# Prompt attention interleaved over four tiles, the routing table made on TensorE, and w_in asked in the phase before

## The chip, the cores and the metric

One core of one Trainium2 chip runs the whole program. The metric is the device time of one execution in microseconds; lower is better. PE is TensorE, DVE VectorE, ACT ScalarE, POOL GpSimd, and SP issues transfers.

## What is computed

One inference step of a trunk of two layers, for a prompt of 2048 tokens and eight samples of one token. Layer 0 is sparse attention: an indexer of 8 heads scores every earlier key, each query keeps its 256 best keys, and 16 query heads over 4 key heads attend to those. Layer 1 is a recurrent block. A mixture of experts follows each: of 4 groups one is chosen, in it 2 of 8 experts. Everything is f32. Cut to what the change touches:

```python
def indexer_scores(qi, wi, ki, q_pos, k_pos):
    dots = jnp.einsum('bqhd,bsd->bqhs', qi, ki)
    s = jnp.einsum('bqhs,bqh->bqs', jax.nn.relu(dots), wi * IDX_SCALE)
    return jnp.where(k_pos[None, None, :] <= q_pos[None, :, None], s, -jnp.inf)
# per block of 128 queries: _, idx = lax.top_k(sc, 256); attention over k[idx], v[idx] only

def dispatch_experts(x, eidx, ew, w1, w2):   # eidx: two experts per token
    order = jnp.argsort(flat_e)
    padded = (counts + blk - 1) // blk * blk          # each expert filled up to blocks of 128
    dest = pstart[se] + (jnp.arange(A) - start[se])
    row_tok = jnp.full((nb * blk,), N, jnp.int32).at[dest].set(st)
    xb = x_pad[row_tok].reshape(nb, blk, D)           # rows by block, gathered
```

## The kernel before

The program is a chain of phases, each a block in which the five queues run their own instruction lists in order and meet by semaphores; a barrier stands between two phases. The order is `phase_modulation`, `phase_project`, `phase_attend`, `phase_sample_index`, `phase_sample_attend`, then for layer 0 `phase_route`, `phase_experts`, `phase_combine`, then `phase_recurrent`, then the last three again for layer 1.

`phase_modulation` (L133) multiplies the condition with 12 slabs of 2 MB of `ada_w` (SP asks them at L170, four buffers). `phase_project` (L258) multiplies 17 tiles of 128 tokens with `w_in`; POOL asks for that weight at L312 as the phase opens, while SP asks for the modulation, the rope table (L299, L300), a gain and then the tiles x (L306).

`phase_attend` (L484) treats 16 tiles of 128 queries in order; tile t sees 128(t + 1) keys. No key is gathered: the indexer's score is kept for all keys, a search by bits (31 counts over the row, `counted`, L752) finds the 256th largest, and a bf16 row `hide` of 0 or a large negative number is added to the logits through a product with an identity. One turn of the loop for tile t has these parts, and each queue holds them in this order:

- *maxima*: PE makes the logits in bf16 (L838 adds `hide`, L839 the product) for 16 heads in units of up to 1024 keys, in two halves of `big` (four PSUM banks); DVE takes the maximum of each (L788), then `negmax` (L790).
- *index of tile t + 1*: PE turns the index queries (L812) and makes dots in pairs of pieces of up to 512 keys (L820) into the two banks of `dots`; ACT rectifies (L649), DVE weighs and adds to `score` (L724, L728). DVE first runs `normalise(t - 1)` (L710, L712).
- *projection of tile t - 1*: PE, 32 instructions (L909) into `big`; ACT copies (L694), POOL multiplies by the gate, adds x and stores.
- *turning the queries of tile t + 1* (L901), copied by ACT (L658) and narrowed to bf16 by POOL (L594).
- *products of tile t*: PE takes two blocks of 128 keys at a time, each for the 4 heads of one key head: `hide` and `negmax` by products (L866, L867), the f32 logits (L872), two blocks later the product with V (L887) into `po` or `dots`. ACT takes the exponential (L681). ACT copies results out in `copy_out` (L674).
- beside them DVE runs the *search of tile t + 1*; the mask (L743, L745) waits until the products of tile t have read the old `hide`.

`phase_route` (L1345) norms each token tile, multiplies with the router and, when all are done, DVE computes for each token its two places in the list sorted by expert (`dest`, L1610). POOL writes the token numbers to `row_tok` in DRAM with 34 indirect transfers (L1464). `phase_experts` (L1671) loads that list back (L1745), casts it (L1807), turns it on PE (L1875) and copies it (L1809); from it POOL gathers the rows of each block (L1752).

## Time and profile before

| | |
|---|---|
| median of 3 runs | 6822.19 us (6815.61 to 6827.62) |
| the profiled execution | 6845.33 us |
| its span, first to last instruction | 6843.7 us |
| PE, PE weight loads, DVE, ACT, POOL busy | 74%, 36%, 41%, 21%, 10% |
| mean granted clock of TensorE | 0.823 |
| DMA | 634 MB, mean 93 GB/s |

A row of a table of stretches gives a stretch in us from the span's start, its length, for each of PE, PE weight loads, DVE, ACT and POOL the busy us with the instructions in brackets, then the mean granted clock, the busy share of the DMA engines and GB/s. A row of a timeline gives start, length, engine (SPq is SP's queue), line, operation, output and inputs, shape, how many instructions are merged, and in square brackets the idle time of that engine before it and what ended it. Matmul ends are modelled; the distance between two starts is the surer figure.

### The profile page before, as it was taken

What the parts mean: (1) busy time and instruction counts of PE and PEld (TensorE: products, weight loads), DVE (VectorE), ACT (ScalarE), POOL (GpSimd) and SP (SyncE); (2) the same over time, 40 slices, a digit from 0 to 9 for tenths busy, and PEclk for the clock granted to TensorE, in tenths of its full rate; (3) what the DMA queues carried; (4) which work ended last, traced back from release to release, by engine and by line L of the source; (5) the groups of instructions that cost most, each with busy time, mean ns of one, the idle gap of its engine ahead of it and who ended that gap; (6) DMA issues with size and microseconds to landing.
All of it is one profiled execution on the core that took longest, in us unless ns stands there. A gap on an engine that the chain in (4) does not pass through costs nothing. (4 is left out here: it accounts for less than half of the span.)

```text
span 6843.7 us, 59514 instructions
## 1 busy us (share of the span) xinstructions
PE 5063.8 (74%) x16273; PEld 2487.8 (36%) x16274; DVE 2836.4 (41%) x5054; ACT 1432.4 (21%) x2686; POOL 714.1 (10%) x943
## 2 busy tenths in 40 slices
PE   6999678888888888874376479962888886559970
PEld 1444223222223322322033334432656565424430
DVE  1111688866677786501812301114444442311014
ACT  0111222222222222220021112211323221212221
POOL 0111110000000000000021210111000000120013
PEclk8999788877799888985687589985899896579985
DMA  6111100000000000003243567754010000437865
GB/s 224 54 50 38 64 12 22 11 12 11 11 11 11 11 11 7 7 8 106 81 146 106 204 227 282 269 213 173 19 37 18 31 19 11 147 105 256 293 225 165
DMA packets 197327, 634.38 MB, mean 93 GB/s; under 512 B 49533, under 2 KB 68353, under 8 KB 178572
## 3 DMA queue, kind: packets, MB, share of 16 engines
q1 hardware_dynamic: 129454, 404.10, 17.2%
q0 software_dynamic: 41888, 136.49, 5.9%
q10 hardware_dynamic: 25824, 91.88, 3.3%
q8 instruction: 72, 1.18, 0.1%
q14 instruction: 89, 0.73, 0.0%
HBM read 497.55 MB, written 134.89 MB: 92 GB/s over the span
## 5 line engine op out<-in xcount | busy, mean ns | idle before, releaser
L1861 PE MATMUL experts_ps_gu<-w_sb,experts_xT 128*128 x1504 | 682.5, 608 | 42.1 <-DMA w_sb<-moe_w_in 37.7
L752 DVE TENSOR_SCALAR_CACHE_REDUCE attend_relu<-attend_score,attend_cand 128x384 f32<-128x384 f32 (+13 forms) x448 | 662.7, 1479 | 43.4 <-issue 3.1
L2373 PE MATMUL recurrent_psAB<-recurrent_hT,rec_w_in_sb 128*128 128x256 f32 (+1 forms) x2304 | 536.1, 392 | 10.6 <-ACT recurrent_hT L2168 10.6
L468 PE MATMUL project_pj<-project_w,project_hT 128*128 128x512 f32 (+2 forms) x1360 | 507.9, 531 | 6.6 <-ACT project_proj L384 5.5
L2373 PEld LDWEIGHTS recurrent_psAB<-recurrent_hT,rec_w_in_sb 128*128 128x128 f32 x2304 | 463.7, 215 | 76.9 <-issue 11.7
L681 ACT ACTIVATE attend_PT<-attend_big 128x512 f32<-128x512 f32 x544 | 297.1, 595 | 631.0 <-PE attend_big L872 629.9
L1861 PEld LDWEIGHTS experts_ps_gu<-w_sb,experts_xT 128*128 128x128 f32 x1504 | 286.2, 195 | 373.2 <-issue 373.2
L820 PE MATMUL attend_dots<-kiT,attend_qiT 64*128 64x512 f32 (+3 forms) x640 | 267.2, 930 | 202.8 <-ACT attend_relu L649 191.8
L838 PE MATMUL attend_big<-attend_hide,attend_identb 128*128 128x512 bf16 (+3 forms) x640 | 259.1, 406 | 180.1 <-DVE attend_mx L788 94.2
L788 DVE TENSOR_REDUCE attend_mx<-attend_big 128x1 f32<-128x1024 f32 (+7 forms) x384 | 334.4, 909 | 126.2 <-PE attend_big L839 121.8
L1851 PE MATMUL experts_ps_y<-w_sb,experts_midT 128*128 x752 | 343.1, 599 | 11.4 <-issue 11.4
L1815 DVE SCALAR_TENSOR_TENSOR experts_th<-experts_th,experts_ps_gu 128x256 f32<-128x256 f32 x94 | 39.6, 421 | 731.1 <-ACT experts_th L1789 731.1
L468 PEld LDWEIGHTS project_pj<-project_w,project_hT 128*128 128x128 f32 (+1 forms) x1360 | 229.5, 185 | 262.0 <-issue 254.9
L872 PE MATMUL attend_big<-attend_qT,KT 64*128 64x512 f32 x1088 | 307.2, 641 | 0.0
L887 PE MATMUL attend_po<-attend_PT,V 128*128 128x512 f32 x544 | 269.8, 618 | 0.0
L909 PE MATMUL attend_big<-attend_w_out,attend_oT 128*128 128x512 f32 x512 | 253.2, 657 | 20.2 <-DVE attend_oT L712 20.2
L887 PE MATMUL attend_dots<-attend_PT,V 128*128 128x512 f32 x544 | 266.0, 615 | 0.0
L2404 PE MATMUL recurrent_psO<-rec_w_out_sb,recurrent_g 128*128 128x512 f32 (+1 forms) x544 | 240.0, 602 | 28.9 <-DVE recurrent_g L2330 28.9
L728 DVE SCALAR_TENSOR_TENSOR attend_score<-attend_relu,attend_wi,attend_score 128x512 f32<-128x512 f32 (+3 forms) x280 | 187.4, 671 | 165.4 <-ACT attend_relu L649 146.7
L839 PE MATMUL attend_big<-attend_KTb,attend_qTb 128*128 128x512 bf16 (+3 forms) x640 | 252.2, 406 | 0.0
L649 ACT ACTIVATE attend_relu<-attend_dots 128x512 f32<-128x512 f32 (+3 forms) x320 | 154.8, 531 | 317.7 <-PE attend_dots L820 260.2
L820 PEld LDWEIGHTS attend_dots<-kiT,attend_qiT 64*128 64x128 f32 x640 | 74.3, 283 | 385.4 <-ACT attend_relu L649 369.7
(372 smaller groups left out, 6285.5 us busy)
## 6 DMA issues: line engine op xcount, KB each, us to landing
w_sb<-moe_w_in SPq DMA_DIRECT2D x64, 2048.0 KB, 11.8
w_sb<-moe_w_in SPq DMA_DIRECT2D x64, 1024.0 KB, 8.7
yb_scratch<-experts_y ACTq DMA_DIRECT2D x94, 512.0 KB, 8.6
modulation_slab<-ada_w_in SPq DMA_DIRECT2D x12, 2048.0 KB, 9.4
index_slab<-ada_w_in SPq DMA_DIRECT2D x12, 2048.0 KB, 8.2
sample_V<-cache_v_in POOLq DMA_DIRECT2D x128, 128.0 KB, 2.4
sample_K<-cache_k_in SPq DMA_DIRECT2D x128, 128.0 KB
route_x<-xa_scratch SPq DMA_DIRECT2D x32, 512.0 KB, 4.5
```

The lines of the kernel that those rows point to most:

```text
L468: last = pe.matmul(pj[0:rows, bank, 0:c1 - c0], hT[:, b, k, 0:rows], w[:, k, c0:c1], start=(k == 0), stop=(k == KC - 1))
L681: act.activation(PT[:, k % 4, :], big[:, k % 4, :], ACT.Exp).then_inc(exped, 1)
L752: dve.tensor_scalar(relu[:, :, :].rearrange("p a n -> p (a n)")[:, 0:w], score[:, 0:w], bound, 0.0, op, ALU.add, accum_out=count[:, :])
L788: dve.tensor_reduce(mx[:, h, u:u + 1], flat[:, 1024 * (k % 2):1024 * (k % 2) + wide], AX.X, ALU.max).then_inc(maxed, 1)
L820: pe.matmul(dots[:, k % 2, 0:keys.stop - keys.start], qiT[r, h // 2, :], kiT[r, keys], start=True, stop=True).then_inc(dotted, 1)
L838: pe.matmul(bank, identb4[:, 0, :], hide[:, keys], start=True, stop=False)
L872: pe.matmul(big[:, k % 4, :], KT[r, n // 2, b * P:(b + 1) * P], qT[r, t % 2, n // 2 * GQ:(n // 2 + 1) * GQ, :].rearrange("p a q -> p (a q) ...
L887: pe.matmul(out_bank(n), V1[:, b, n, :], PT[:, k % 4, :], start=(b == 0), stop=(b == per - 1)).then_inc(pv_done, 1)
L909: last = pe.matmul(big[:, 2 + half, :], oT[:, k, :], w_out[:, k, half * 512:half * 512 + 512], start=(k == 0), stop=(k == KC - 1))
L1851: last = pe.matmul(ps_y[:, half, :], midT[:, k, :], w2[:, bass.ds(slot, 1), k, half * 512:half * 512 + 512].rearrange("p a n -> p (a n)"), ...
L1861: last = pe.matmul(ps_gu[:, u, :], xT[:, u, k, :], w1[:, bass.ds(slot, 1), k, :].rearrange("p a n -> p (a n)"), start=(k == 0), stop=(k == ...
L2373: last = pe.matmul(psAB[:, c % 2, part, 0:W], w_in[:, k, part * D + c * P:part * D + (c + 1) * P], hT[:, k, 0:W], start=(k == 0), stop=(k ...
```

## The change

- **Attention.** The tiles are taken in the order 0, 1, 3, 5, ... 15, 14, 12, ... 2. Step i of the new loop (`steps`, -3 to 16) holds four tiles: the products of the i-th, the maxima of the next, the search of the one after, the index dots of the third. The step is divided in slots of two product blocks (`slots`, 2(t + 1) of them). Units of the maxima, now 512 keys wide in the two banks `aux`, are dealt over the first half of the slots, pairs of index pieces over the second half, and 33 rounds of the search over all; in the middle slot stand the normalising and projection of the tile before and the turning of index queries, behind the last slot the turning of queries. `hide` has three buffers, `score` and `diag` two, `qT` three. `aux` serves maxima, turning, dots and projection; `po` all products with V. The count of the search writes its elements to the bf16 tile `passed`. `qi_rows` and `q_rows` of the first tile are asked before `w_out`, and all engines wait for the constants first.
- **w_in.** The weight has a tile that lives through modulation and projection, and SP asks for it behind the last slab. Three of the four slabs lie in `V1` and `KT`.
- **Routing table.** DVE splits each place into block and row, marks both as 0 or 1 (times the token number), and PE multiplies 34 pairs of marks, which sums to the table of token numbers by row and block; DVE copies it to `idx`, which stays in SBUF. The `row_tok` list, its fill, scatters, load and turn go, in both layers.

```diff
@@ phase_modulation
+        slab = [pair[:, 0], pair[:, 1], T["KT"]..., slab3[:, :, :]]
+                for k in range(KC):
+                    sp.dma_start(T["project_w"][:, k, :], T["attn_w_in"][k * P:(k + 1) * P, :]).then_inc(T["project_w_in"], 16)
@@ phase_project
-                for k in range(KC):
-                    pool.dma_start(w[:, k, :], T["attn_w_in"].rearrange("(k p) n -> p k n", p=P)[:, k, :]).then_inc(w_in, 16)
-                    pool.wait_ge(w_in, 16 * KC)
@@ phase_attend
+        TILE = [0] + list(range(1, NT, 2)) + list(range(NT - 2, 0, -2))
+        ROUNDS = 33
+        def steps():
+            return range(-3, NT + 1)
+        def slots(i):
+            return S[i] // 2 if there(i) else 1
+        def share_of(n, s, first, last):
+            if not first <= s < last:
+                return range(0)
+            s, of = s - first, last - first
+            return range(n * s // of, n * (s + 1) // of)
+        def units_at(i, s):
+            return share_of(U[i + 1], s, 0, max(middle(i), 1)) if there(i + 1) else range(0)
+        def pairs_at(i, s):
+            return share_of(I[i + 3] // 2, s, middle(i), slots(i)) if there(i + 3) else range(0)
...
 # scalar
+                for i in steps():
+                    for s in range(slots(i)):
+                        if there(i):
+                            exponentials(i, s)
+                        if s == 0 and there(i - 1):
+                            copy_out(i - 1, 1)
+                        if s == middle(i):
+                            if there(i - 1):
+                                take_projection(i - 1)
+                            if there(i):
+                                copy_out(i, 0)
+                            if there(i + 3):
+                                take_index_queries(i + 3)
+                        for pair in pairs_at(i, s):
+                            rectify(i + 3, pair)
+                    if there(i + 2):
+                        take_queries(i + 2)
 # vector
-                    dve.tensor_scalar(relu[:, :, :].rearrange("p a n -> p (a n)")[:, 0:w], score[:, 0:w], bound, 0.0,
-                                      op, ALU.add, accum_out=count[:, :])
+                    dve.tensor_scalar(passed[:, 0:L[m]], score[:, m % 2, 0:L[m]], bound, 0.0, op, ALU.add, accum_out=count[:, :])
+                for i in steps():
+                    for s in range(slots(i)):
+                        for u in units_at(i, s):
+                            largest(i + 1, u)
+                        if s == middle(i):
+                            if there(i - 1):
+                                normalise(i - 1)
+                            if there(i + 3):
+                                scale_weights(i + 3)
+                        for pair in pairs_at(i, s):
+                            add_up(i + 3, pair)
+                        if there(i + 2):
+                            for r in share_of(ROUNDS, s, 0, slots(i)):
+                                search(i + 2, r)
 # tensor
+                def fill(m, u):
...
+                    if u == 0:
+                        pe.wait_ge(qTb_ready, 2 * (m + 1))
+                        pe.wait_ge(hidden, m + 1)
+                    pe.wait_ge(maxed, sum(U[:m]) + u + 1)
+                    pe.matmul(aux[:, u % 2, 0:n], identb4[:, 0, :], hide[:, m % 3, keys], start=True, stop=False)
+                    pe.matmul(aux[:, u % 2, 0:n], qTb[:, h, :], KTb[:, h // GQ // 2, keys], start=False, stop=True).then_inc(unit_filled, 1)
+                def project(i):
+                    pe.wait_ge(maxed, 2 + sum(U[:i + 3]))
...
+                    pe.wait_ge(o_normed, i + 1)
...
+                for i in steps():
+                    for s in range(slots(i)):
+                        if there(i):
+                            biased, scored_by_keys
+                        if s:
+                            with_values
+                        for u in units_at(i, s):
+                            fill(i + 1, u)
+                        if s == middle(i):
+                            if there(i - 1):
+                                project(i - 1)
+                            if there(i + 3):
+                                turn_index_queries(i + 3)
+                        for pair in pairs_at(i, s):
+                            index(i + 3, pair)
+                    if there(i + 2):
+                        turn_queries(i + 2)
@@ phase_route
-                        pool.indirect_dma_start(out=T["row_tok"], out_offset=bass.IndirectOffsetOnAxis(ap=dest_i[0:rows, t, k:k + 1], axis=0),
-                                                in_=token[0:rows, t:t + 1], in_offset=None).then_inc(scattered, 16)
+                dve.tensor_scalar(split_i[:, 0, :], flat_i, BLK - 1, None, ALU.bitwise_and)
+                dve.tensor_scalar(split_i[:, 1, :], flat_i, 7, None, ALU.logical_shift_right)
+                dve.tensor_copy(split_f[:, :, :], split_i[:, :, :])
+                dve.tensor_tensor(in_block[:, :, :], split_f[:, 1, :]..., columns(0, 2 * NTT, NBR), ALU.is_equal)
+                dve.tensor_tensor(in_block..., in_block..., token_f..., ALU.mult).then_inc(placed, 1)
+                for first, last in ((0, NTT), (NTT, 2 * NTT)):
+                    dve.tensor_tensor(in_row[:, first:last, :], row_number(first, last), columns(first, last, P), ALU.is_equal).then_inc(rows_marked, 1)
+                dve.wait_ge(slots_done, 1)
+                dve.tensor_copy(T["idx"][:, :], psR[:, 0, 0:NBR])
+                pe.wait_ge(placed, 1)
+                for k in range(2 * NTT):
+                    if k % NTT == 0:
+                        pe.wait_ge(rows_marked, k // NTT + 1)
+                    last = pe.matmul(psR[:, 0, 0:NBR], in_row[:, k, :], in_block[:, k, :], start=(k == 0), stop=(k == 2 * NTT - 1))
```

## Rows read from the trace of the kernel before

**Rows 1.** Table of stretches by phase: length, busy us (instructions) per engine, clock, DMA share, GB/s.
```profile
102.00:142.60 40.60, 1.94 (x8) 1.57 (x8) 4.95 (x4) 2.19 (x4) 8.76 (x11) 0.50 0.79 300
697.70:3045.00 2347.30, 1929.68 (x5888) 693.06 (x5888) 1626.17 (x2692) 611.89 (x1232) 175.75 (x96) 0.85 0.04 13
3905.60:3961.90 56.30, 0.37 (x1) 0.18 (x1) 5.59 (x9) 0.00 (x0) 35.31 (x37) 0.50 0.17 63
6010.00:6067.00 57.00, 0.38 (x1) 0.18 (x1) 5.95 (x10) 0.00 (x0) 35.31 (x36) 0.50 0.02 1
```

**Rows 2.** The same table for the stages of one tile of attention.
```profile
2632.00:2684.00 52.00, 31.78 (x65) 7.86 (x62) 29.36 (x35) 17.23 (x32) 3.60 (x1) 0.54 0.00 0
2702.00:2815.00 113.00, 113.00 (x354) 40.37 (x352) 83.03 (x115) 36.58 (x71) 5.16 (x5) 1.00 0.03 10
2819.40:2857.20 37.80, 31.98 (x125) 9.46 (x122) 37.70 (x32) 0.00 (x0) 0.00 (x0) 1.00 0.00 0
```

**Rows 3.** Timeline of PE, one slot of products: start us, length us, then the instruction.
```profile
2900.61 0.38 PE L866 MATMUL attend_big<-attend_identb,attend_hide 128*128 128x512 bf16 x1
2901.56 1.13 PE L872 MATMUL attend_big<-attend_qT,KT 64*128 64x512 f32 x4
2902.62 1.98 PE L887 MATMUL attend_po<-attend_PT,V 128*128 128x512 f32 x4
2904.44 0.38 PE L866 MATMUL attend_big<-attend_identb,attend_hide 128*128 128x512 bf16 x1
```

**Rows 4.** Groups by form on DVE, attention: busy us, mean ns | idle us before.
```profile
L788 DVE TENSOR_REDUCE attend_mx<-attend_big 128x1 f32<-128x512 f32 x32 | 21.3, 685 | 2.2 <-PE attend_big L839 1.6
L728 DVE SCALAR_TENSOR_TENSOR attend_score<-attend_relu,attend_wi,attend_score 128x512 f32<-128x512 f32 x196 | 147.1, 751 | 142.3 <-ACT attend_relu L649 129.2 <-DVE attend_score L728 1.4
```

**Rows 5.** Timeline of DVE, two counts and the end of a search.
```profile
2778.30 2.35 DVE L752 TENSOR_SCALAR_CACHE_REDUCE attend_relu<-attend_score,attend_cand 128x2048 f32<-128x2048 f32 x1
2781.21 2.35 DVE L752 TENSOR_SCALAR_CACHE_REDUCE attend_relu<-attend_score,attend_cand 128x2048 f32<-128x2048 f32 x1
2783.64 1.29 DVE L772 TENSOR_SCALAR attend_ties<-attend_score,attend_cand 128x2048 bf16<-128x2048 f32 x1
2789.63 2.29 DVE L777 SCALAR_TENSOR_TENSOR attend_ties<-attend_passed,attend_ties 128x2048 bf16<-128x2048 bf16 x1
```

**Rows 6.** Timeline of PE, one pair of index pieces.
```profile
2447.90 2.08 PE L820 MATMUL attend_dots<-kiT,attend_qiT 64*128 64x512 f32 x4 [1.17 <-ACT attend_relu L649]
```

**Rows 7.** Timeline of DVE and PE, a normalising and the last projection.
```profile
2857.35 6.54 DVE L710 RECIPROCAL attend_total<-attend_total 128x1024 f32<-128x1024 f32 x1
3016.84 16.35 PE L909 MATMUL attend_big<-attend_w_out,attend_oT 128*128 128x512 f32 x32 [10.76 <-DVE attend_oT L712]
```

**Rows 8.** Timeline of ACT, one of the eight copies of a pair of heads.
```profile
3005.66 0.38 ACT L674 ACTIVATE attend_total<-attend_dots 64x256 f32<-64x256 f32 x1
```

**Rows 9.** Timeline of PE and POOL at the start of attention.
```profile
697.72 0.72 PEld L812 LDWEIGHTS attend_dots<-ident,attend_qi_rows 128*128 128x128 f32 x4 [27.80 <-DMA attend_qi_rows<-qs_scratch]
687.09 1.79 POOL L607 MEMSET attend_qTb<- 128x2048 bf16 x1
```

**Rows 10.** Table of stretches, modulation.
```profile
90.00:100.00 10.00, 7.74 (x19) 1.46 (x16) 1.36 (x2) 0.00 (x0) 0.00 (x0) 0.99 0.02 4
```

**Rows 11.** Timeline of POOL and SP's queue at the start of the projection.
```profile
102.41 4.49 POOL L312 DMA_DIRECT2D project_w<-attn_w_in_in  x8 [100.52 <-POOLq L83]
105.57 20.41 SPq L300 DMA_DIRECT2D project_rope<-rope_in  x1
```

**Rows 12.** Timeline of POOL, the first scatter and the first gather.
```profile
3906.04 2.92 POOL L1464 DMA_INDIRECT row_tok_scratch<-route_token,dest  x1 [46.77 <-DVE dest L1610]
3961.89 1.04 POOL L1752 DMA_INDIRECT experts_x<-hs_scratch,experts_idxb  x1 [0.93 <-POOL experts_idxb L1749]
```

**Rows 13.** Timeline of PE, small f32 products in the route phase.
```profile
3830.61 3.47 PE L1646 MATMUL route_psL<-route_wr,route_hT 128*128 128x36 f32 x16
```

**Rows 14.** Table of stretches, the maxima of tile 9.
```profile
1604.00:1655.00 51.00, 36.58 (x96) 11.77 (x97) 24.20 (x33) 1.10 (x3) 0.00 (x0) 0.51 0.00 0
```

## What the change is forecast to do

> **What bounds the kernel now.** I read the table of stretches first: the program is a row of phases, and a step is worth what its own phase lets it be worth. Prompt attention (697.7 to 3045) takes 2347 us of 6844, with PE busy 1930, DVE 1626 and a granted clock of 0.85 [rows 1]. The 40.6 us before the first projection product and the 56.3 us before the first gather of the experts (57 us in the second layer) hold almost no compute [rows 1]. Other phases only start earlier.
>
> Then one tile of attention (key tile 14, 225 us), cut by stage [rows 2]. The reader should see four parts in which one engine waits for another: index dots 52 us (clock 0.54, PE busy 32, DVE 29), output projection up to 2702, products 113 at clock 1.00 with the search of the next tile beside them, maxima 38 (DVE busy 37.7). So products hide the search, and nothing hides dots and maxima. These 90 us of a large tile are what an interleaving can win.
>
> **Attention, priced.** Units of work:
> - A slot of two product blocks costs PE 3.83 us at full clock (2900.61 to 2904.44) [rows 3]; there are 272.
> - Maxima are now cut in units of 512 keys: 640 units against 384 reduces. A reduce costs DVE 0.685 us at 512 keys [rows 4]; passes of one element a cycle grow by 0.00104 us per key (0.751 at 512 [rows 4], 2.35 at 2048 [rows 5]), so a piece costs 0.15 by itself. PE needs 0.43 to 0.48 a unit (four bf16 products up to 2901.56 in 0.95 [rows 3]).
> - A search round on DVE is p = 0.77 + 0.00104 per key: 2.91 us at 2048 (2778.30 to 2781.21) [rows 5]. The end of a search is 10.7 us up to the mask [rows 5] and some 3.2 for the mask (the stretches leave 4.4 us between products and maxima [rows 2]): 1.8 + 0.006 per key.
> - The count now writes bf16 instead of f32; no row shows that form. The comparison without count that writes bf16 takes 1.29 us at 2048, the counting one 2.35 [rows 5]. By the first, 450 counts at a mean of 1216 keys would fall by some 0.6 us each, 270 us of DVE; the nearest row that counts is the second, so I take no gain, and keep 0 to 100 us for the range (half of the steps are not bound by DVE).
> - A pair of index pieces costs DVE 2 x 0.75 [rows 4] and PE 1.06 at full clock, as the same four 64-row products do in a slot (2901.56 to 2902.62) [rows 3]; now it takes 2.08 + 1.17 us by the handshake at half clock [rows 6].
> - Normalising is 6.5 us and a product of the same width, 7.9 together. The projection after a wait of 10.8 us takes 16.35 [rows 7], where 32 starts of 0.43 would be 13.7. I take 16.0.
>
> Queues run in order, so stalls come from what stands behind a wait. A step of the new loop, by these rules:
> 1. First half: a slot holds q units and about 33/n rounds (n slots in the step). PE: 3.83 + 1.2 + 0.685(q - 2), since two banks of `aux` hold the units and the third fill waits for a reduce that waited for the first fill. DVE: 0.2 + 0.685q + rounds x p. A slot costs the larger. Tile 15 (q = 4, one round of 2.5): 6.4 against 5.5, 16 slots, 102 us. Tile 7 (q = 6 with short pieces, two rounds of 2.37): DVE 8.5, 8 slots, 68 us.
> 2. Middle: PE stands at `project(i - 1)` and DVE only now runs `normalise(i - 1)`: 7.9 us of idle PE, then 16.0 us of projection in which DVE stands at `add_up`. On ACT `take_projection`, `copy_out(i, 0)` with eight copies of 0.38 [rows 8] and the take of the index queries stand before the first `rectify`: 0.6 + 3.2 + 0.6 and latencies, 4.7. Head: 28.6 us where DVE is the bound or the middle slot has a pair, else 23.9. Before, DVE went on searching beside the projection.
> 3. Second half: PE slots x 3.83 + pairs x 1.06 (a second pair in a slot waits for ACT, 2.5); DVE pairs x 1.6 + rounds x p; the larger sum. Tile 15: 70 (PE). Tile 7: 62 (DVE).
> 4. End: the last slot holds two rounds and the end of the search behind the last `add_up`, and slot 0 of the next step fills only after `hidden`. PE waits 6 to 17 us, with one slot of products under it.
>
> Steps of tiles 0, 1, 3, 5, 7, 9, 11, 13, 15, 14, 12, 10, 8, 6, 4, 2 come to 68, 112, 133, 150, 171, 191, 209, 215, 211, 200, 171, 150, 121, 97, 68, 43; 45 fill the pipeline before them, 24 are the last projection and 12 its residual and store. Sum 2391 against 2347 now: **+44** (own bounds -60 and +110: all waits at full clock, or slots of 4.2 us). The engines' work alone, the larger of PE and DVE in each step, is 1994. Steps up to tile 11 are DVE-bound, because the search is two tiles larger than the products beside it; the other 400 us are heads, ends and handshakes. That is why four stages side by side win so little.
>
> **Attention's first data.** `qi_rows` is now asked before the 4 MB of `w_out`. It holds PE until 697.7; POOL's constants, for which all now wait, end at 688.9 [rows 9]: **-9** (bounds -10, -4).
>
> **w_in early.** DMA moves 4 GB/s from 90 to 100 us [rows 10]. The 8.7 MB of `w_in` (1024 x 2120 x 4 bytes) are asked on POOL at 102.4, and SP then stands 20.4 us at L300 before it can ask for x [rows 11]. After: SP asks it behind the last slab (near 71 us), 25 to 30 us of transfer end near 105. The slabs stand ahead of it; the stores of `mods` share its engines, 0 to 3 us. L300 then waits only for the 2048 rows of 128 bytes of `rope`: bounds 0.4 (an issue) and 20.4 (now), I take 3, and all behind it comes as much earlier: **-18** (bounds -24, -5). The Trainium skill, page "DMA: Bandwidth & Descriptors", Specifications, says transfers under 512 bytes miss the line rate; by it the rope rows alone would still hold SP for several us, and the gain would be nearer 12.
>
> **Routing table.** From the cast of `dest` (3905.6) to the first gather (3961.9) stand 34 scatters, a barrier, a load and a turn [rows 1, 12]. After: DVE splits and copies (1.1 us), two passes over 2312 elements (2.5 each) and two over 2176 (2.4 each) by the price per element above: PE may start 8.4 us after the cast and has its second half at 10.7. 34 f32 products are 68 instructions; after idling 16 take 3.47, 0.217 each [rows 13], half of that at full clock, so 8 to 15 us, I take 13. 21.5 after the cast the table is there; copy 0.3, barrier 2.5, gather issue 1.3, and 1.9 since the first indirect DMA of a phase takes 2.92 where the gather took 1.04 [rows 12]: 27.5. 56.3 - 27.5 = 29 in each layer: **-58** (bounds -66, -48). The plan's two passes of DVE lie beside PE. POOL's added constants, some 1.5 us, lie under the loads at the phase's start, and the lost fill of `row_tok` was hidden.
>
> Sum: +44 - 9 - 18 - 58 = -41. The profiled execution took 6845.3 (span 6843.7 and 1.6 around it) and gives 6804; it lies 23 us above the median of the runs, so against 6822.2 the forecast is **6781**.
>
> **The clock, weighed.** After a wait of 10.8 us the projection takes 16.35 us instead of 13.7, and the dots run at 0.54 [rows 2, 7]: nearer 1.2 GHz after waits, 2.4 after work. I put 2.3 us in each head and 2.5 in the longer ends, some 55 in all. The Trainium skill, "TensorE: Matmul & The Clock Gate", Part 1, says that throttled is the default state and activity releases it. By it the dots gain most from the interleaving, and each wait listed above is paid once more behind it; without that attention would be 2335.
>
> **Rivals.**
> - *The stalls overlap after all.* If heads and ends lie under queued work, attention nears 1994. With two thirds of the 400 us recovered it is 2125, in all 6515 (6430 to 6640). For it: PE 1930 and DVE 1626 leave room [rows 1]. Against: in the middle each engine waits for the other's next instruction, and queues do not reorder. 0.13.
> - *Slower: PE stays at half clock in the growing steps.* In steps of tiles 1 to 13 PE has work for 60 to 80% of the time. The maxima of tile 9 ran at clock 0.51 for 51 us with DVE busy only 24 [rows 14], those of tile 15 at 1.00 [rows 2]. At half clock a product slot is 7.7, PE becomes the bound from tile 3 on: +5, 16, 29, 40, 54, 68 for tiles 3 to 13, and 11.7 for each of seven projections, 295 in all: 7076. With tiles up to 7 alone it is +97: 6878. [...] 0.17.
> - *No change.* The barriers and first DMAs eat half of the gains at start and route (-43 instead of -85) beside attention's +44: 6823. 0.12.
> - *Forecast*, 6700 to 6850: 0.58.
>
> **Chances.** About 0.2% (14 us) can be told from no change. Forecast case: 0.47 faster, 0.04 same, 0.07 slower. Overlap: 0.13 faster. Half clock: 0.02 same, 0.15 slower. No change: 0.03 faster, 0.07 same, 0.02 slower. Faster 0.63, same 0.13, slower 0.24. The range 6600 to 6900 leaves out most of the overlap case and the full half-clock case, 0.2 together; the forecast's own is 6700 to 6850.
>
> **What would show it.** Route: table copied 22 us after the cast, gather within 30. Start: first projection product at 122 to 128 us. Attention: PE idle 8 us before each projection, DVE idle 20 us behind it, PE waiting for the mask at slot 0; slots of 6.4 and 4.9 us at tile 15. The prediction is wrong if a count of 2048 keys takes under 2 us, if the projection finds its operand ready, or if slots at tiles 5 to 11 show clock 0.5.

## The result, and the profile after

The changed kernel takes **6894.06 us** (median of 4 runs, 6885.89 to 6895.11) against 6824.32 for the kernel before on the same chip: ratio 1.0097, 95% interval 1.0085 to 1.0109. By the ratio it is 66 us slower where 41 us faster were forecast. The time lies inside the range of 6600 to 6900, at its upper end, but outside the forecast case's own 6700 to 6850, and on the side that had a chance of 0.24. The spans of the profiled executions are 6893.2 and 6843.7.

The stretches of the changed kernel that answer to [rows 1] (length, busy us and instructions of PE, PEld, DVE, ACT, POOL, then clock, DMA share, GB/s): from the start of the projection phase to its first product, attention, and the two ways from the cast of `dest` to the first gather.

```profile
98.00:122.30 24.30, 1.94 (x8) 1.57 (x8) 5.04 (x5) 2.21 (x4) 4.26 (x3) 0.59 0.48 143
660.20:3160.70 2500.50, 1880.50 (x5788) 666.78 (x5888) 1653.36 (x2948) 608.33 (x1232) 184.72 (x106) 0.88 0.04 14
4018.70:4046.00 27.30, 14.75 (x68) 14.58 (x68) 15.77 (x15) 0.00 (x0) 0.19 (x1) 0.50 0.31 125
6091.80:6119.60 27.80, 14.74 (x68) 14.58 (x68) 15.69 (x15) 0.00 (x0) 0.23 (x2) 0.50 0.00 1
```

Three of the four are as forecast: the first projection product stands at 122.3 (122 to 128 were given), and route needs 27.3 and 27.8 us instead of 56.3 and 57.0. Attention is the fourth. Its block, first to last instruction and barrier, was 2363.5 us (681.7 to 3045.2) and is 2500.5: +137 where +35 was forecast (+44 and the -9 of its first data). PE is busy for 1880 us where it was for 1930, DVE for 1653 where it was for 1626 [rows 1]: most of the 137 us went into waits. (The trace has 5788 of PE's products where it has 5888 weight loads, so PE's busy time is too short by what the missing 100 took.)

The longest waits of DVE in attention (engine, its line, whom it waited for: us in total, times, longest us):

```profile
DVE attend_score L774 <- ACT attend_relu L711: 300.1, 33, 24.1
DVE attend_mx L751 <- PE attend_aux L891: 208.6, 221, 21.7
DVE attend_total L758 <- ACT attend_total L689: 72.3, 2, 41.3
DVE attend_score L778 <- ACT attend_relu L711: 69.5, 52, 3.6
```

and those of PE in one step, key tile 15:

```profile
PE attend_aux L890 <- issue: 12.3, 1, 12.3
PE attend_aux L902 <- DVE attend_oT L760: 8.8, 1, 8.8
PE attend_aux L890 <- DVE attend_mx L751: 5.3, 15, 0.4
```

The first row of DVE is mostly the middle of the steps: `add_up` waits for `relu`, which waits for dots, which stand behind the projection. The two large waits of PE are in slot 0 and before the projection. The timeline names what the first one waits for, though the row says "issue": DVE's last pass over the mask ends at 2032.14, and PE's first fill starts at 2032.24 (start us, length us, instruction, then the idle time before it):

```profile
2031.48 0.66 DVE L829 TENSOR_SCALAR attend_hide<-attend_hide 128x1920 bf16<-128x1920 bf16 x1
```

```profile
2032.24 0.59 PE L890 MATMUL attend_aux<-attend_hide,attend_identb 128*128 128x512 bf16 x1 [12.32 <-issue]
```

The middle of the same step, DVE, then PE, then ACT:

```profile
2127.09 2.54 DVE L751 TENSOR_REDUCE attend_mx<-attend_aux 128x1 f32<-128x512 f32 x4 [1.07 <-PE attend_aux L891]
...
2130.07 1.95 DVE L786 TENSOR_SCALAR_CACHE_REDUCE attend_passed<-attend_score,attend_cand 128x1664 bf16<-128x1664 f32 x1
...
2133.58 6.54 DVE L758 RECIPROCAL attend_total<-attend_total 128x1024 f32<-128x1024 f32 x1
2140.20 1.23 DVE L760 TENSOR_TENSOR attend_oT<-attend_oT,attend_total 128x1024 f32<-128x1024 f32 x1
```

```profile
2129.73 1.13 PE L869 MATMUL attend_big<-attend_qT,KT 64*128 64x512 f32 x4
2130.79 1.98 PE L880 MATMUL attend_po<-attend_PT,V 128*128 128x512 f32 x4
2141.57 3.75 PE L902 MATMUL attend_aux<-attend_w_out,attend_oT 128*128 128x512 f32 x4 [8.80 <-DVE attend_oT L760]
```

```profile
2158.21 0.60 ACT L698 ACTIVATE attend_y<-attend_aux 128x512 f32<-128x512 f32 x1 [6.27 <-PE attend_aux L902]
2158.70 0.36 ACT L689 ACTIVATE attend_oT<-attend_po 64x256 f32<-64x256 f32 x1
...
2161.91 0.60 ACT L702 ACTIVATE attend_qiT<-attend_aux 128x512 f32<-128x512 f32 x1
```

DVE comes to the reciprocal after the last reduces and one round, PE idles 8.8 us, the projection runs to 2158, ACT makes eight copies, and only then do the index queries follow. That is the head that the prediction priced at 23.9 (28.6 where DVE bounds).

The steps, from the first product of a tile to that of the next, in us:

```
tile              0    1    3    5    7    9   11   13   15   14   12   10    8    6    4
forecast         68  112  133  150  171  191  209  215  211  200  171  150  121   97   68
changed kernel   53  131  149  149  179  199  215  222  217  205  176  157  129  107   72
its clock       .63  .67  .75  .86  .88  .88  .90  .92  .94  .94  .96  .93  .93  .92  .93
e7 (all three)   78   98  143  128  173  180  196  199  194  182  157  139  114   94   69
e10 (17 rounds)  42  104  121  133  160  177  198  212  214  202  174  154  126  104   70
```

The 15 steps miss the forecast by 93 us in sum, the fill of the pipeline by 7 (first product 59.1 us after the block's start, 52 forecast) and the end by 2.

### The profile page after: what moved, and what is told of

It is laid out like the page before. It is cut to its first block and busy times, and to the rows that moved or that the text cites. A ratio compares the mean times of both kernels' runs of the same rounds, so it can differ in the third digit from the quotient of the medians.

```text
span 6893.2 us, 59882 instructions
## 1 busy us (share of the span) xinstructions
PE 5034.6 (73%) x16307; PEld 2487.0 (36%) x16408; DVE 2883.1 (42%) x5322; ACT 1427.6 (21%) x2686; POOL 645.6 (9%) x871
## 5 line engine op out<-in xcount | busy, mean ns | idle before, releaser
L786 DVE TENSOR_SCALAR_CACHE_REDUCE attend_passed<-attend_score,attend_cand 128x512 bf16<-128x512 f32 (+13 forms) x448 | 662.6, 1479 | 45.9 <-issue 2.1
L880 PE MATMUL attend_po<-attend_PT,V 128*128 128x512 f32 x1088 | 541.7, 621 | 8.5 <-ACT attend_total L689 8.5
L751 DVE TENSOR_REDUCE attend_mx<-attend_aux 128x1 f32<-128x512 f32 (+3 forms) x640 | 365.7, 606 | 219.4 <-PE attend_aux L891 208.6
L890 PE MATMUL attend_aux<-attend_hide,attend_identb 128*128 128x512 bf16 (+3 forms) x603 | 230.1, 384 | 256.6 <-issue 129.0
L902 PE MATMUL attend_aux<-attend_w_out,attend_oT 128*128 128x512 f32 x512 | 258.6, 669 | 155.5 <-DVE attend_oT L760 155.5
L880 PEld LDWEIGHTS attend_po<-attend_PT,V 128*128 128x128 f32 x1088 | 184.9, 189 | 353.8 <-issue 351.9
L891 PE MATMUL attend_aux<-attend_KTb,attend_qTb 128*128 128x512 bf16 (+3 forms) x640 | 244.2, 387 | 37.2 <-issue 33.4
L930 PE MATMUL attend_aux<-kiT,attend_qiT 64*128 64x512 f32 (+3 forms) x640 | 182.4, 651 | 100.2 <-ACT attend_relu L711 75.5
L890 PEld LDWEIGHTS attend_aux<-attend_hide,attend_identb 128*128 128x128 bf16 x640 | 63.9, 100 | 502.2 <-DVE attend_mx L751 274.3
L863 PE MATMUL attend_big<-attend_diag,attend_onesb 128*128 128x512 bf16 x544 | 223.8, 411 | 8.3 <-issue 6.7
```

Source lines behind the costliest of these rows:

```text
L751: dve.tensor_reduce(mx[:, h, c:c + 1], aux[:, u % 2, 0:wide], AX.X, ALU.max).then_inc(maxed, 1)
L786: dve.tensor_scalar(passed[:, 0:L[m]], score[:, m % 2, 0:L[m]], bound, 0.0, op, ALU.add, accum_out=count[:, :])
L880: pe.matmul(po[:, n % 2, :], V1[:, b, n, :], PT[:, g % 4, :], start=(b == 0), stop=(b == S[i] // NKV - 1)).then_inc(pv_done, 1)
L890: pe.matmul(aux[:, u % 2, 0:n], identb4[:, 0, :], hide[:, m % 3, keys], start=True, stop=False)
L891: pe.matmul(aux[:, u % 2, 0:n], qTb[:, h, :], KTb[:, h // GQ // 2, keys], start=False, stop=True).then_inc(unit_filled, 1)
L902: last = pe.matmul(aux[:, half, :], oT[:, k, :], w_out[:, k, half * 512:half * 512 + 512], start=(k == 0), stop=(k == KC - 1))
```

## The experiments

Ratios are to the kernel before on the same chip, whose median was 6828 to 6830 us in these comparisons; differences to the changed kernel are taken between ratios and given in us of 6824.

**e1, attention put back.** `phase_attend` of the kernel before in the changed kernel, nothing else.

> The changed kernel with its attention phase put back to the serial one of before; the routing table on TensorE and the early load of the projection weights stay. Theory A (the attention phase alone turned the sum, it costs 137 us in the profiled executions and the other two parts gave what was forecast): 6824 - 58 - 21 = about 6745, some 150 us below the changed kernel. Theory B (the parts are not independent; the early parts only shift work into other waits once the attention is serial again): 6790 or more.

Measured 6762.92 us, ratio 0.9898 (0.9876 to 0.9919): 136 us below the changed kernel. Theory A holds. The attention phase alone turned the sum, and without it the change would have been a gain of 70 us (55 to 85), where the prediction's two other terms made 76.

**e2, the routing table alone.**

```diff
-                pool.wait_ge(scattered, 16 * 2 * NTT)
...
+                    last = pe.matmul(psR[:, 0, 0:NBR], in_row[:, k, :], in_block[:, k, :], start=(k == 0), stop=(k == 2 * NTT - 1))
```

> The kernel before with the routing table on TensorE alone; loads and attention as before. By the prediction's term 58 us less than before, 6766 (bounds 6758 to 6776). If the gain belongs partly to the other parts (a shorter route only lets the expert weights arrive late), it is under 30 us. The difference between this run and the one with both other parts is the early load of the projection weights: 18 by the prediction, 21 by the trace.

Measured 6778.3 us, ratio 0.9916 (0.9892 to 0.9940): -57 us (-73 to -41), next to the forecast 58, though the interval is wide. e1 lies 12 us lower, which would be the early `w_in`, but each of the two intervals is 15 to 16 us to either side, so the times alone don't show this term. The traces do: the first projection product stands at 121.4 in e1 and at 142.7 in e2, 21 us apart, where 18 were forecast.

**e3, the normalisation spread.** `parts_at` deals the eight parts of 128 columns over the slots from 1 to the one ahead of the middle.

```diff
+                        if there(i - 1):
+                            for k in parts_at(i, s):
+                                normalise(i - 1, k)
                         if s == middle(i):
-                            if there(i - 1):
-                                normalise(i - 1)
```

> The changed kernel with the normalisation of the previous tile cut in eight parts and dealt over the first half of the step, so that the output projection finds its operand ready. Theory A (PE stands 8 to 15 us before each of 15 projections because VectorE reaches the reciprocal only in the middle, and nothing runs beside that): 8 to 12 us less in each of the seven steps that TensorE bounds (tiles 15 to 4) and 2 to 5 in the eight that VectorE bounds, 90 us in all, about 6805. Rival (the waits only move: the parts delay the reduces, TensorE waits for those instead): within 20 us of the changed kernel, 6875 to 6895.

Measured 6824.84 us, ratio 0.9993 (0.9982 to 1.0003): 71 us less than the changed kernel, where theory A gave 90 and the rival under 20. The projection of the step of tile 15:

```profile
2108.26 13.97 PE L909 MATMUL attend_aux<-attend_w_out,attend_oT 128*128 128x512 f32 x32 [1.17 <-DVE attend_oT L760]
```

The wait of 8.80 is 1.17, and the projection takes 13.97 instead of 16.6: two gains at one place, and the step is 10 us shorter (206.9). In the steps of tiles 5, 7 and 11 next to nothing is gained (148.5, 179.0, 215.1): DVE's wait for `relu` is 4 to 6 us shorter there, but cut in eight the normalisation keeps DVE busy some 4 us longer.

**e4 and e8, PE kept busy in the gap.** 24 products that nobody reads ahead of the wait, in e8 44.

```diff
+                    for k in range(24):
+                        pe.matmul(aux[:, k % 2, :], identb4[:, 0, :], identb4[:, :, :].rearrange("p a q -> p (a q)"), start=True, stop=True)
                     pe.wait_ge(o_normed, i + 1)
```

> The changed kernel with 24 extra bf16 products (128x512, results never read) that TensorE runs just before it waits for the normalised output, so that it is busy in the gap before each projection. They take about 9 to 10 us at full clock, less than the gap of 10 to 15 us. If the clock after an idle gap is what makes projection and first dots slow, each projection falls from 16.3 to about 14 us and the dots behind it run at full clock: 30 to 50 us less, about 6850. If the projection's 16.3 us is its own pace, nothing changes (6894) or it grows by a few us where the extra products outlast the gap (tiles 1 and 3 run them at half clock).

> The changed kernel with 44 unread bf16 products before the wait for the normalised output. The 24 of the run before took 0.22 us each and left 3.5 us of the gap open, and the projection kept its 15.4 to 17 us, while it took 13.9 in the one step where nothing was left open. 44 fill 9.7 us, the whole gap in the steps of tiles 11 to 10. If idle time just before the projection is what costs the clock, the projection falls to 13.9 us in these six steps, 14 us in all for the kernel, about 6880. If not, the projection stays at 16 and the time at 6894 or above.

Measured 6899.6 us (ratio 1.0091, 1.0069 to 1.0112) and 6897.74 (1.0095, 1.0077 to 1.0113): both as the changed kernel. e4's price for the extra products was wrong: 24 took 5.34 us, not 9 to 10, and left 3.52 of the gap. PE at tile 15, e4 and then e8 (whose first row is cut off by the start of the view and has the last 28 of the 44; together they take 9.66 us from 2127.59 on):

```profile
2132.86 5.34 PE L900 MATMUL attend_aux<-attend_identb 128*128 128x512 bf16 x24
2141.72 16.77 PE L904 MATMUL attend_aux<-attend_w_out,attend_oT 128*128 128x512 f32 x32 [3.52 <-DVE attend_oT L760]
```

```profile
2130.83 6.42 PE L900 MATMUL attend_aux<-attend_identb 128*128 128x512 bf16 x28
2137.09 13.90 PE L904 MATMUL attend_aux<-attend_w_out,attend_oT 128*128 128x512 f32 x32
```

So the prediction's price for the idle gap is there: with the gap filled a projection takes 13.9 us, and in the changed kernel it takes 15.5 to 17.0, 1.6 to 3.1 more. The granted clock in the first 4 us of this projection is 0.50 in the changed kernel and in e4, and 1.00 in e8 (stretches of e4, then e8):

```profile
2141.72:2145.70 3.98, 3.98 (x5) 1.85 (x6) 2.29 (x5) 0.00 (x0) 0.00 (x0) 0.50 0.00 0
2137.10:2141.00 3.90, 3.90 (x11) 1.75 (x10) 1.81 (x4) 0.00 (x0) 0.00 (x0) 1.00 0.01 4
```

The Trainium skill, "TensorE: Matmul & The Clock Gate", Part 1, says that activity releases the throttle; the trace agrees (13.90 against 16.77).

To buy it back in this way gains nothing that the times can tell. In e8's profiled execution the steps of tiles 15 to 6 are 10 us shorter in sum, and that of tile 2, which had no gap and a projection of 13.9 us already, is 9.5 longer; attention as a whole is 7 us shorter, less than two intervals of 8 and 12 us to either side can tell.

**e5, rounds in the middle.** `rounds_at` counts the middle slot as 1 + slots // 4 slots, so that 7 to 13 of the 33 rounds of a step run in it, ahead of `add_up`.

```diff
+                        if there(i + 2) and s == middle(i):
+                            for r in rounds_at(i, s):
+                                search(i + 2, r)
                         for pair in pairs_at(i, s):
                             add_up(i + 3, pair)
```

> The changed kernel with 7 to 13 of the 33 search rounds moved into the middle slot, ahead of the first add_up, where VectorE now idles about 20 us per step beside the projection and ScalarE's copies. All other rounds keep their order. Theory A (the steps of tiles 1 to 11 are bound by VectorE, which stands 20 us in the middle for nothing): 15 to 20 us less in each of six steps, some 8 in tile 13, and 2 in each later one (one round less behind the last add_up): 100 to 140 us in all, about 6775. Rival (TensorE at a low clock bounds these steps): under 40 us, 6855 or more.

Measured 6813.64 us, ratio 0.9974 (0.9962 to 0.9986): 84 us less. Below A's 100 to 140, but more than twice the rival's 40. The steps of tiles 3 to 11 lost 12, 8, 9, 10 and 14 us where 15 to 20 each were expected, that of tile 13 lost the expected 8. That of tile 1 lost 32 and that of tile 0 grew by 26: search rounds that had run behind its `add_up`, into tile 1's first slot, now run ahead of it.

**e6, the mask early.** The rounds are dealt over all but the last eighth of the slots.

```diff
-                            for r in share_of(ROUNDS, s, 0, slots(i)):
+                            for r in rounds_at(i, s):
```

> The changed kernel with the rounds dealt over all but the last eighth of the slots, so that the mask of the next tile but one is written before the step ends. Theory A (in the steps that TensorE bounds it stands at slot 0 for the mask, 7 to 14 us beyond a slot): 5 to 12 us less in each of seven steps, nothing in the steps that VectorE bounds (its work is the same): 50 to 60 us, about 6840. Rival (denser rounds delay the reduces of the first half, which return the gain): under 20 us, 6875 or more.

Measured 6873.45 us, ratio 1.0065 (1.0044 to 1.0086): 22 us less, between the two theories. The steps of tiles 15 to 6 fell by 6 to 10 us each, 47 in all, as A said, while those of tiles 3 and 7 grew by 17 and 11. The rival's mechanism isn't shown by that growth: DVE is busy 14 and 12 us longer in these two steps, because the end of a search (at tile 3 five counts too) that had run behind them now lies in them. A said that nothing would change in the steps bound by DVE; up to tile 11 they are 25 us longer in sum, and why that much isn't shown.

**e7, e3, e5 and e6 together.**

> The changed kernel with the normalisation spread, the rounds in the middle slot and the mask early, all three. If the three stalls are separate, the gains add: 70 (measured for the first) + 120 + 50 = 240, about 6650 (6600 to 6700), faster than the kernel before (6824) and than the one with the serial attention (6763). If they are one and the same wait seen three times, it comes to 6750 or more.

Measured 6688.71 us, ratio 0.9794 (0.9777 to 0.9811): 207 us less than the changed kernel, **faster than both kernels** and than e1. The single gains make 177, so the stalls are separate; the 30 us beyond the sum are hardly clear of the four intervals. 240 were expected from 70, 120 and 50, where the single runs gave 71, 84 and 22. Steps of tile 9 and tile 15, as in the stretches above:

```profile
1339.90:1520.10 180.20, 143.45 (x438) 48.29 (x445) 155.20 (x235) 49.30 (x96) 10.96 (x6) 0.93 0.03 11
1914.40:2108.20 193.80, 183.45 (x593) 63.94 (x604) 152.33 (x243) 56.73 (x112) 10.97 (x6) 0.99 0.03 10
```

In the changed kernel these two steps were

```profile
1380.50:1579.30 198.80, 147.16 (x438) 49.20 (x445) 152.94 (x227) 49.23 (x96) 10.99 (x6) 0.88 0.03 10
2016.10:2232.90 216.80, 187.18 (x594) 65.03 (x605) 150.32 (x230) 56.79 (x112) 10.96 (x6) 0.94 0.03 9
```

The work is the same but for the parts of the normalisation, idle PE at tile 15 falls from 29.6 to 10.4 us, and the clock rises to 0.99.

**e9, index queries first.** e7 with one more edit on ACT.

```diff
+                            if there(i + 3):
+                                take_index_queries(i + 3)
                             if there(i):
                                 copy_out(i, 0)
-                            if there(i + 3):
-                                take_index_queries(i + 3)
```

> The kernel with the three edits together (6689 measured) and one more: in ScalarE's middle slot the copy of the turned index queries comes before the eight copies of the attention output, not behind them. Between the projection's end and that copy stand 3.7 us in each of 13 steps, in which TensorE waits where it is the bound. Theory A (the eight copies are on the path): 3 us less in each of 13 steps, 40 us in all, 6650. Rival (the copies come later instead, and the first product of the second value bank waits for them): 6680 to 6700.

Measured 6678.31 us, ratio 0.9780 (0.9767 to 0.9793). Against e7 that is 10 us, inside the intervals: the rival in the main. PE behind the projection of tile 15:

```profile
2030.27 2.46 PE L899 MATMUL attend_po<-attend_PT,V 128*128 128x512 f32 x4 [1.94 <-ACT attend_total L698]
2032.66 2.08 PE L949 MATMUL attend_aux<-kiT,attend_qiT 64*128 64x512 f32 x4
```

The V product waits for the copies now (1.94 us), and the first dots come 7.8 us after the projection instead of 5.8. The steps of tiles 15 to 6 grew by 2 to 3 us each, those of tiles 1, 3, 9 and 13 fell by 1 to 5; attention as a whole is as long as in e7 (2285 and 2281 us in the profiled executions), so the 10 us aren't shown to be its.

**e10, seventeen rounds.** `ROUNDS = 17`.

> The changed kernel with 17 rounds of search in place of 33 (it leaves out the 16 lowest bits of the threshold, so too many keys pass; every other operation runs as before). Theory A (the steps up to tile 11 are bound by VectorE, as the prediction's table has them): by the same table with 17 rounds the steps of tiles 0 to 11 fall by 21, 26, 25, 23, 14, 17 and 13 us and the rest by 1 or 2: 142 us in all, about 6752. Rival (these steps are bound by TensorE at a low clock and by the waits between the engines): 50 us or less, 6845 or more.

Measured 6718.75 us, ratio 0.9839 (0.9824 to 0.9854): 176 us less than the changed kernel, more than the 142 of theory A, three times the rival's. DVE bounded the steps up to tile 11. With half of the search out of the way the table's rules hold to 6 us at tiles 5 to 11 (127, 157, 174 and 196 by the table less the falls expected, 133, 160, 177 and 198 measured), are missed by 18 and 13 at tiles 1 and 3 (86 and 108 by the table), and the steps of tiles 15 to 4, which PE bounds, stay 3 to 9 us longer than the table.

**e11, tiles in their own order.** `TILE = list(range(NT))`.

> The changed kernel with the tiles in their natural order 0 to 15 in place of 0, 1, 3 ... 15, 14 ... 2. The same step rules give 2452 us for attention in place of 2385: the last two steps have nothing to search or to dot beside them and the growing steps are all bound by VectorE with 28 us heads: +67, about 6961. If the small growing steps are what the changed kernel loses on (each search and each index is two tiles larger than the products beside it), the natural order, where they are one and two tiles larger, costs less than that or gains: 6900 or below.

Measured 6951.49 us, ratio 1.0176 (1.0161 to 1.0192): 54 us more than the changed kernel, 67 expected. The up-and-down order is a gain, and the step rules priced this edit to 13 us.

**e12, the normalisation on GpSimd.** A power of -1 and a product on POOL, the first work of POOL in a step; rounds and mask as in e7.

```diff
+                    pool.tensor_tensor(total[:, :, :], total[:, :, :], minus[:, :, :].broadcast_to([P, KC, P]), ALU.pow)
+                    pool.drain()
+                    pool.tensor_tensor(oT[:, :, :], oT[:, :, :], total[:, :, :], ALU.mult).then_inc(o_normed, 1)
```

> The kernel with the rounds in the middle slot and the mask early (as in the three edits together, 6689 measured), but with the whole normalisation on GpSimd, which idles for most of each step: a power of -1 over 128 x 1024 and a product (2.35 us as its other passes of that size), issued as the first work of the step. VectorE loses 7.9 us of work per step. Theory A (the power takes GpSimd under some 20 us; the seven steps that VectorE bounds fall by 8 us each, in the others the reduces of the first half come 0.5 us earlier per slot): 60 to 90 us less, about 6615. Rival (the power is so slow on GpSimd that it outlasts the first half of the step, 25 us at tile 1 and 100 at tile 15, so that projection and GpSimd's copies of the maxima wait for it): 6700 or more.

Measured 8463.73 us, ratio 1.2402: the rival, and far beyond its price. The groups of POOL (busy us, mean ns):

```profile
L673 POOL TENSOR_TENSOR attend_total<-attend_total,attend_minus 128x1024 f32<-128x1024 f32 x16 | 2613.0, 163315 | 55.5 <-ACT attend_total L710 55.4 <-issue 0.2
...
L675 POOL TENSOR_TENSOR attend_oT<-attend_oT,attend_total 128x1024 f32<-128x1024 f32 x16 | 37.7, 2355 | 2.3
```

## Why the prediction was wrong

**Right: the parts outside attention.** Route: 27.3 and 27.8 us for 27.5. The 34 products took 14.7 us for 13, and the first gather stood 3.9 us behind the table's copy for 6.0, since the 1.9 us added for the first indirect DMA of the phase didn't come (it took 1.11). That the sum is met within half a microsecond is luck: the errors are small and cancel. The start: 18 forecast, 21 by the traces. SP stands 3.28 us at the rope table now, where 20.41 us were spent before and the prediction took 3; the smaller gain of 12, which the prediction gave beside its sum for a slow transfer of these rows, didn't come:

```profile
104.80 3.28 SPq L306 DMA_DIRECT2D project_rope<-rope_in  x1
```

The first index transposition stands 7.2 us after the block's start instead of 16.0, the -9 of that term.

**Right: what the loop does.** Every mark named at the end of the prediction is there: PE idle before each projection (8.8 us at tile 15), DVE idle behind it, PE without the mask at slot 0, slots of tile 15 of 6.2 and on average 4.7 us (6.4 and 4.9 forecast). The bf16 target gave nothing, as taken. The count before and after:

```profile
L752 DVE TENSOR_SCALAR_CACHE_REDUCE attend_relu<-attend_score,attend_cand 128x384 f32<-128x384 f32 (+13 forms) x448 | 662.7, 1479 | 43.4 <-issue 3.1
```

```profile
L786 DVE TENSOR_SCALAR_CACHE_REDUCE attend_passed<-attend_score,attend_cand 128x512 bf16<-128x512 f32 (+13 forms) x448 | 662.6, 1479 | 45.9 <-issue 2.1
```

**Wrong: the size of the steps**, 93 us too small in sum. The rules that failed are rule 2, the middle, in the steps that PE bounds (tiles 13 to 4), which miss by 51 us; rule 1, the first half, in those of tiles 5 to 11, which DVE bounds and which miss by 21; and the whole table at tiles 0, 1 and 3, 20. Read from the traces:

- *The middle slot, 47 of the 51.* From the start of the middle slot to the start of the next one PE takes 30.8 us at tile 15, where rule 2 has 23.9; over the eight steps the excess is 47. At tile 15 it is made of four terms. The largest was put at nothing: rule 1 counts the slots ahead of the middle, rule 3 those behind it (16 and 15 of 32), and the products of the middle slot itself, 3.83 us, run ahead of the projection and are in neither, 31 us over the eight steps. That is an error of counting. The others are the gap (8.8 us for 7.9), the projection (16.6 for 16.0), and 1.4 us behind it for ACT's last copy and the turning of the index queries.
- The path through this stretch is DVE's. From PE's last fill to the projection stand 12.8 us, in which PE has 4 us of products and then idles; DVE ends its last reduce, does `negmax` and a round (together 3.9 us in the steps of tiles 11, 13, 15, 14 and 12) and only then the 7.8 us of normalising. The prediction let DVE come to the normalisation as soon as PE came to the projection. e3 takes this wait away (1.17 us left), and the step of tile 15 falls by 10.
- *DVE in the first half, about 25.* 0.2 us per slot was put down for its waits for fills. At tiles 5, 7, 9 and 11 they are 3.6, 5.5, 8.5 and 14.9 us, 25 more in sum than the rule has. At tile 9, ten slots:

```profile
DVE attend_mx L751 <- PE attend_aux L891: 8.5, 12, 2.0
```

 A slot has either more rounds or fewer, and PE's products hold up the first fill of it; then the larger of two sums is a lower bound where two engines hand over in each slot. That is a reading of the rows, no run tests it. The steps of tiles 7, 9 and 11 came 8, 8 and 6 us later, that of tile 5 met its forecast, so something gave a few us back.
- *The steps of tiles 0, 1 and 3, 20 in sum* (-15, +19, +16). The clock is 0.63 to 0.75 there and the dots go back and forth with ACT. e10 takes half of the search away and leaves +18 and +13 at tiles 1 and 3, so it isn't the search. Which share is the clock's wasn't separated: e8 took 2.5 us off tile 3 and nothing off tile 1.

The fill of the pipeline was 7 us longer. The index queries of the second tile are asked at 668.7, behind the 4 MB of `w_out` that are asked from 662.05 on, and land 10.4 us later, where the loads of this kind before and after it took 2.7 and 2.6. PE stood 5.0 us for them; the rest isn't assigned:

```profile
679.12 1.11 PE L918 MATMUL attend_aux<-ident,attend_qi_rows 128*128 128x128 f32 x4 [5.02 <-DMA attend_qi_rows<-qs_scratch]
```

The prediction put the first load ahead of the weights and did not look at the second.

With the products of the middle slot alone counted the sum would have been -10 instead of -41, no change that can be told. No single instruction of attention was priced far off; a forecast that is the difference of two large phases (2391 against 2347) carries each small error sixteen times.

**The rivals.** PE at half clock through the growing steps did not come: the clock is 0.86 to 0.92 from tile 5 to 13, and e10 shows that DVE bounds the steps up to tile 11. Only the steps of tiles 0 to 3 come near it (0.63 to 0.75). The overlap of the stalls did not come by itself, but e7 shows that it was to be had: 207 of the changed kernel's some 500 us above the 1994 of the engines' work alone, by moving three pieces of DVE's work in its queue.

## What to carry to other kernels

When streams are interleaved by hand, look for the places where every engine waits for the next instruction of another: here the normalisation and the projection in the middle slot, and the mask at slot 0. Put the long independent work (search rounds) in front of the instruction that must wait, and have a result ready a few slots before its reader comes; that turned a loss of 66 us into a gain of 141. In a forecast by steps, count the slots of a step once against the loop bounds before anything is priced, and where two engines meet, ask what each still has in its queue ahead of the meeting.

## What the runs showed of the hardware

A power on GpSimd over 128 x 1024 f32 takes 163.3 us, 0.16 us per element of a partition; the product over the same tile takes 2.36 and VectorE's reciprocal 6.54. Under 20 were expected.

The projection of 32 products takes 13.9 to 14.0 us where the granted clock is 1.00 in its first 4 us, and 15.4 to 17.0 where it is 0.50 to 0.67 there. In the 14 steps of the changed kernel in which PE idled 4.9 to 20.3 us before it, it took 15.5 to 17.0; with no gap in e8, and with 0.2 to 1.3 us in e3 and e7 at tiles 15 to 8, 13.9 to 14.0. The length of the gap alone doesn't tell: in e3 2.25 and 2.47 us before the projections at tiles 4 and 6 were followed by 15.67, and 3.73 at tile 3 by 13.97. Nor does the want of a gap: in the kernel before, 14 projections had none and took 14.7 to 16.6, most of them behind index dots that ran at clock 0.50. In e4, with 3.4 to 3.6 us left open in six steps (tiles 11, 13, 15, 14, 12 and 10), these projections took 15.8 on average where the changed kernel's took 16.3.

24 bf16 products of 512 columns that follow each other without a wait take 5.34 us, 0.22 each, while a single one is shown with 0.38: what a row gives as the length of one instruction isn't the pace of a row of them.
